# A chunked recurrence on one Trainium2 core: where among a head's scores the next head's decay sums are computed, when the logs are rounded, and which engine takes the queries out of PSUM

## The reference, cut to what matters

```
log_f = logaddexp(log(lb), log1p(-lb) + log_sigmoid(z))     # per token and key dimension
k = (1 - lb) * sigmoid(-z);   q, v from the projection
b = cumsum(log_f)                                            # inside a chunk
A[t, s] = sum_k q[t, k] * k[s, k] * exp(b[t, k] - b[s, k])   # s <= t
o = (q * exp(b)) @ S + A @ v
S = exp(b_last) * S + (k * exp(b_last - b))^T @ v
```

## Time and profile before

| | before |
|---|---|
| median of three runs | 3051.93 us |
| profiled execution, its own time | 3050.5 us |
| its span, first to last instruction | 3048.5 us |
| TensorE busy (matmul) | 3003.0 us, 99% |
| VectorE busy | 1624.6 us, 53% |
| ScalarE busy | 1112.0 us, 36% |
| GpSimd busy | 59.5 us, 2% |
| mean granted TensorE clock | 0.996 |
| chain that ended last | PE 84%, DVE 9%, ACT 5% |

### The profile page before, as it was taken

How to read it: one execution, slowest core, us unless ns; L and a number is a source line. 1 busy time by engine, 2 the same in 40 slices (tenths; PEclk the granted TensorE clock), 3 DMA queues, 4 the chain that set the end, 5 groups by cost and what they waited for, 6 DMA issues and landing times.

```text
span 3048.5 us, 33745 instructions
## 1 busy us (share of the span) xinstructions
PE 3003.0 (99%) x14426; PEld 2479.1 (81%) x14426; DVE 1624.6 (53%) x1880; ACT 1112.0 (36%) x1321; POOL 59.5 (2%) x68
## 2 busy tenths in 40 slices
PE   8999999999999999999999999999999999999998
PEld 6888878888888888888788888888888888788886
DVE  4555555556545466464544555554465564545445
ACT  5535445354322236333432223322236334422222
POOL 0000000000000000200000000000000200000000
PEclk9999999999999999999999999999999999999999
DMA  4121221212233223113222222222232023222221
GB/s 146 52 83 46 88 96 42 83 49 97 97 105 112 97 100 110 41 56 137 81 98 93 93 95 96 97 97 97 97 112 101 22 83 125 82 97 94 90 94 68
DMA packets 41925, 270.56 MB, mean 89 GB/s; under 512 B 5776, under 2 KB 6032, under 8 KB 10544
## 3 DMA queue, kind: packets, MB, share of 16 engines
q1 hardware_dynamic: 41776, 268.40, 25.5%
HBM read 266.22 MB, written 2.10 MB: 88 GB/s over the span
## 4 chain that ended last, share of the span: by engine, by line
PE 84%; DVE 9%; ACT 5%; issue 1%; DVEq 1%; DMA 0%; SPq 0%; ACTq 0%
PE PS L245 24%; PE PS L247 24%; PE PS L246 24%; DVE w_lo L230 4%; ACT w_hi L222 3%; DVE XT L1521 2%; PE PS L2061 1%; PE PS L1145 1%; PE PS L1278 1%; PE PS L652 1%; PE PS L2307 1%; PE PS L2338 1%; PE PS L2041 1%; PE PS L1267 1%; PE PS L710 1%
## 5 line engine op out<-in xcount | busy, mean ns | idle before, releaser
L222 ACT ACTIVATE w_hi<-w_raw 128x2048 fp32r<-128x2048 f32 x241 | 461.3, 1914 | 1202.2 <-PE PS L247 1200.2
L230 DVE TENSOR_TENSOR w_lo<-w_raw,w_hi 128x2048 fp32r<-128x2048 f32 x241 | 552.2, 2291 | 381.8 <-ACT w_hi L222 380.8
L245 PE MATMUL PS<-uh_b,w_hi 128*128 128x512 f32 x1312 | 511.7, 390 | 0.0
L247 PE MATMUL PS<-uh_b,w_lo 128*128 128x512 f32 x1312 | 510.6, 389 | 0.0
L246 PE MATMUL PS<-ul_b,w_hi 128*128 128x512 f32 x1312 | 510.5, 389 | 0.0
L245 PE MATMUL PS<-uh_a,w_hi 128*128 128x512 f32 x800 | 314.0, 393 | 3.6 <-DVE ul_a L572 2.2
L245 PE MATMUL PS<-w_hi,uh_a 128*128 128x512 f32 x768 | 306.1, 399 | 9.2 <-DVE ul_a L305 7.6
L247 PE MATMUL PS<-uh_a,w_lo 128*128 128x512 f32 x800 | 311.4, 389 | 0.0
L246 PE MATMUL PS<-ul_a,w_hi 128*128 128x512 f32 x800 | 311.4, 389 | 0.0
L247 PE MATMUL PS<-w_hi,ul_a 128*128 128x512 f32 x768 | 300.6, 391 | 0.0
L246 PE MATMUL PS<-w_lo,uh_a 128*128 128x512 f32 x768 | 300.5, 391 | 0.0
(11 more groups left out here) (331 smaller groups left out, 3687.9 us busy)
## 6 DMA issues: line engine op xcount, KB each, us to landing
w_raw<-in_weights SPq DMA_DIRECT2D x241, 1024.0 KB, 4.9
XT<-in_xT SPq DMA_DIRECT2D x8, 256.0 KB, 5.9
mem_raw<-in_mem SPq DMA_DIRECT2D x2, 1024.0 KB, 4.8
out<-XT SPq DMA_DIRECT2D x8, 256.0 KB, 2.0
bands<-in_bands SPq DMA_DIRECT2D x2, 768.0 KB, 6.4
mask_numbers<-in_masks SPq DMA_DIRECT2D x1, 1152.0 KB, 8.3
w_raw<-in_weights SPq DMA_DIRECT2D x4, 256.0 KB, 5.3
p_raw<-in_pT SPq DMA_DIRECT2D x2, 512.0 KB, 3.4
```

The source lines that it names most:

```text
L222: act.activation(self.hi[g % 2][:], self.raw[g % 2][:], ACT.Copy).then_inc(self.hi_done.sem, 1)
L230: dve.tensor_tensor(self.lo[g % 2][:], self.raw[g % 2][:], self.hi[g % 2][:], ALU.subtract).then_inc(self.lo_done.sem, 1)
L245: pe.matmul(out, sh, mh, start=first, stop=False)
L247: return pe.matmul(out, sl, mh, start=False, stop=last)
```

## The change

1. **Logs rounded early.** ScalarE rounds the logs inside the projection, after the weight block g0+7 and before it takes `U`, into a new tile `LFhi` that lies where `m.mix` will be. Inside `PoolAndStates` it no longer does so, and VectorE takes the remainder as soon as the last projection block is done.
2. **Queries.** The one VectorE multiplication from PSUM is replaced by four ScalarE copies, one for each bank, and one multiplication from SBUF to SBUF by VectorE after the keys' multiplications. The log sums of chunk c wait for copy c.
3. **Tiles of the coming head's sums among the scores.** Tile 2 of sums(h+1) stands after unit 2 of scores(h), tile 3 after unit 4. Before scores(0) only tiles 0 and 1 of sums(1) are computed; after outputs(h) come turn_keys(h+2) and tiles 0 and 1 of sums(h+2).
4. **States.** VectorE takes the states in the middle of weigh(0), before its fifth level.

```diff
@@ MixerProjection.scalar
         w.split_hi(act, g0 + 7)
+        act.wait_ge(*self.lf.at(1))
+        act.activation(m.LFhi[:, :, 0:DA], m.LF[:], ACT.Copy).then_inc(self.lf_hi.sem, 1)
         w.wait_used(act, g0 + 5)
@@ MixerProjection.vector
         w.split_lo(dve, g0 + 10)
-        w.wait_used(dve, g0 + 9)
-        dve.tensor_tensor(m.Q[:], k.PS[:, 4:8, :], k.R[:].unsqueeze(1).to_broadcast(full), ALU.mult).then_inc(self.qread.sem, 1)
@@ PoolAndStates.scalar
-        act.wait_ge(*self.proj.lf.at(1))
         act.wait_ge(*self.tables.arrived.at(16))
         k.w.wait_used(act, self.proj.g0 + 9)
-        act.activation(uh[:, 0:NT, :], m.LF[:], ACT.Copy).then_inc(self.lf_hi.sem, 1)
-        act.activation(uh[:, 6, 0:P], m.after, ACT.Copy)
-        act.activation(uh[:, 4:6, :].rearrange("p a n -> p (a n)"), m.level, ACT.Copy).then_inc(self.lf_hi.sem, 1)
+        act.activation(uh[:, 6, 0:P], m.after, ACT.Copy).then_inc(self.tables_hi.sem, 1)
+        for h in range(HH):
+            act.activation(m.Q[:, h, :], k.PS[:, 4 + h, :], ACT.Copy).then_inc(self.proj.qread.sem, 1)
+        act.activation(uh[:, 4:6, :].rearrange("p a n -> p (a n)"), m.level, ACT.Copy).then_inc(self.tables_hi.sem, 1)
@@ PoolAndStates.vector
-        dve.wait_ge(*self.lf_hi.at(1))
-        dve.tensor_tensor(self.u[1][:, 0:NT, :], m.LF[:], self.u[0][:, 0:NT, :], ALU.subtract).then_inc(self.lf_lo.sem, 1)
+        dve.wait_ge(*self.proj.lf_hi.at(1))
+        k.w.wait_used(dve, self.proj.g0 + 9)
+        dve.tensor_tensor(self.u[1][:, 0:NT, :], m.LF[:], m.LFhi[:, :, 0:DA], ALU.subtract).then_inc(self.lf_lo.sem, 1)
...
             dve.tensor_tensor(m.Kp[:, c, :], m.Kp[:, c, :], m.K[:, c, :], ALU.mult).then_inc(self.kp.sem, 1)
+        dve.wait_ge(*self.proj.qread.at(HH))
+        dve.tensor_tensor(m.Q[:], m.Q[:], k.R[:].unsqueeze(1).to_broadcast([P, HH, SEQ]), ALU.mult)
+        dve.drain()
@@ PoolAndStates.tensor
-        pe.wait_ge(*self.proj.qread.at(1))
-        pe.wait_ge(*self.lf_hi.at(2))
+        pe.wait_ge(*self.tables_hi.at(1))
         pe.wait_ge(*self.lf_lo.at(1))
         for c in range(NT):
-            pe.matmul(k.PS[:, 4 + c, :], uh[:, 6, 0:P], uh[:, c, :], start=True, stop=False)
+            pe.wait_ge(*self.proj.qread.at(c + 1))
+            pe.matmul(k.PS[:, 4 + c, :], uh[:, 6, 0:P], self.lf_hi_of(c), start=True, stop=False)
@@ Recurrence.vector
             for n in range(LEVELS):
+                if h == 0 and n == 4:
+                    self.states.take_states(dve)
...
         weigh(0)
-        self.states.take_states(dve)
@@ Recurrence.tensor
-        def sums(h):
-            for c in range(NT):
+        def sums(h, tiles):
+            for c in tiles:
...
                 i.then_inc(self.scored.sem, 1)
+                if h + 1 < HH and unit in (2, self.UNITS - 1):
+                    sums(h + 1, (2,) if unit == 2 else (3,))
...
-        sums(0)
+        pe.wait_ge(*self.states.tables_hi.at(2))
+        sums(0, range(NT))
...
-        sums(1)
+        sums(1, (0, 1))
         for h in range(HH):
             scores(h)
-            if h + 2 < HH:
-                turn_keys(h + 2)
...
             outputs(h)
             if h + 2 < HH:
-                sums(h + 2)
+                turn_keys(h + 2)
+                sums(h + 2, (0, 1))
```

More of the change, by code:

```diff
@@ L27 @@
 NH = 8
+PAIRS = NH // 2
 ROPE = 16
@@ L1646, in __init__ @@
         self.lf, self.pooled, self.pool_copied = sig("mixer_lf", 1), sig("mixer_pooled", 4), sig("mixer_pool_copied", 4)
-        self.qread, self.hnorm = sig("mixer_qread", 1), sig("mixer_hnorm", 1)
+        self.qread, self.hnorm, self.lf_hi = sig("mixer_qread", NT), sig("mixer_hnorm", 1), sig("mixer_lf_hi", 1)
     def sync(self, sp):
@@ L1813, in __init__ @@
         self.k, self.m, self.proj, self.u, self.tables = k, m, proj, u, tables
-        self.lf_hi, self.lf_lo, self.state_read = sig("states_lf_hi", 2), sig("states_lf_lo", 1), sig("states_state_read", NT - 1)
+        self.tables_hi, self.lf_lo, self.state_read = sig("states_tables_hi", 2), sig("states_lf_lo", 1), sig("states_state_read", NT - 1)
         self.mapped, self.mapped_read, self.suffix = sig("states_mapped", 4), sig("states_mapped_read", 4), sig("states_suffix", NT)
@@ L1842, in vector, with lf_hi_of @@
             dve.tensor_tensor(m.Kp[:, c, :], m.Kp[:, c, :], m.K[:, c, :], ALU.mult).then_inc(self.kp.sem, 1)
+        dve.wait_ge(*self.proj.qread.at(HH))
+        dve.tensor_tensor(m.Q[:], m.Q[:], k.R[:].unsqueeze(1).to_broadcast([P, HH, SEQ]), ALU.mult)
+        dve.drain()
+    def lf_hi_of(self, c):
+        return self.m.LFhi[:, c, 0:DA]
     def take_states(self, dve):
@@ L2039, in sums @@
                 for half in range(2):
-                    for x in (uh, ul):
-                        i = pe.matmul(k.PS[:, 2 * (c % 2) + half, :], x[:, c, h * P:(h + 1) * P],
-                                      uh[:, 4 + half, :], start=x is uh, stop=x is ul)
+                    bank = k.PS[:, 2 * (c % 2) + half, :]
+                    pe.matmul(bank, self.states.lf_hi_of(c)[:, h * P:(h + 1) * P], uh[:, 4 + half, :], start=True, stop=False)
+                    i = pe.matmul(bank, ul[:, c, h * P:(h + 1) * P], uh[:, 4 + half, :], start=False, stop=True)
                 i.then_inc(self.summed.sem, 1)
@@ L2453, in second_memory @@
     mem.top = at
+    m.LFhi = mem.put("LF_hi", [P, NT, D], F32R)
+    mem.top = at
     m.lb, m.e = mem.put("lb", [P, 2 * DA]), mem.put("lb_exp", [P, 2 * DA])
```

## The result

The changed kernel takes 3079.26 us in the median of four runs (3078.23 to 3081.87), the kernel before 3051.65 in four. The ratio is 1.0093, with a 95% interval from 1.0076 to 1.0111: 27.6 us slower. The forecast was 3072.7, with 20.8 us added to the profiled execution of before, and a range of 3058 to 3084. The execution profiled here took 3081.87 us, the longest of its four, and 31.4 more than the one of before (3050.5).

A forecast was written before the change was run, and what follows sets the result against it. TensorE, busy 99% of the span, was taken as the bound. 13.0 us for two layers plus 9.0 for the clock less 1.2 gave +20.8 on 3050.5, so 3071.3; the median, 1.4 higher, 3072.7; range 3058 to 3084.

The forecast's parts named there:

- Start (edits 1 and 2): Start of the mixer: early rounding and copied queries let the first E come earlier; gain 0.9 us, between 0 and 1.1.
- States (edit 4): Head 0's weighing: with states after four levels, GpSimd finishes beneath them; VectorE needs 8.2 us, not 10.0, gain 1.8.
- The loop on VectorE: Heads 1 to 3: weighing waits for tile 3 and meets GpSimd; periods 16.75 and 17.1 us, +6.5 a layer.
- D: Extra time of a weighing when VectorE and GpSimd multiply SBUF with SBUF together: 4.0 us, head 0 against head 3.
- The clock: TensorE's clock falls behind its 3.4 us idle in heads 1 to 3: 1.5 us each, 9.0 for six, bounds 0 to 3.
- Sum: Whole kernel: 13.0 for two layers, 9.0 for low clock, less 1.2 for the old fall: +20.8 us.
- Range: Whole run: from 3058 us (D 3.3, clock at full level) to 3084 (3 us each fall, larger D in part).
- the clock holds: TensorE in the loop: clock stays up or falls only where TensorE waits anyway; 3063.7 us, chance 0.18.
- the engines don't meet: Weighing in the loop: GpSimd lags or gives way, D is 0, periods 13.2; 3042 us, chance 0.10.
- they meet by half: Weighing in the loop: VectorE wins most turns, D near 2; about 3052 us, no change, chance 0.07.
- blocking rule: Weighings: an undisturbed GpSimd multiplication of 0.73 us is added to each of seven, D 5.1; 3079 us, chance 0.05.

The follow-up runs named there:

- the filled version: Changed kernel with 12, 12 and 18 more 512-column matmuls, results unused, between units 1 and 2 of heads 1, 2 and 3; 3061.25 us, ratio 1.0034.
- GpSimd at three levels: Changed kernel with GpSimd multiplying levels 0 to 2 whole, one column of levels 3 to 6, in heads 1 to 3; 3063.74 us, ratio 1.0050.

## Why the prediction was right, and where its sizes were off

The mechanism and the sign held; that the time came out inside the range is in part luck, as the sum below shows. By the steps of the prediction:

- **Start (edits 1 and 2)**: 0.9 forecast; 1.1 where the clock held. Right, and the rounding cost nothing in its new place: ScalarE's idle ahead of its block there is 4.91 us in place of 6.73.
- **States (edit 4)**: 1.8 forecast on VectorE, and there it is: from the weighing's start to keep 8.0 us (1262.09 to 1270.08), 8.2 forecast, 10.0 before. Without the third edit it is worth 0.07 on the path. With all edits the first outputs of the second layer come 3.3 us earlier than with the tiles alone (26.37 against 29.64), and 1.1 of that is the start's; the 2.1 that are left go to the states by subtraction only, as no run has the tiles and the states without the start. That the two edits lean on each other was not said: the tiles freed TensorE, the states freed VectorE.
- **The loop on VectorE**: keep starts 9.37, 9.74 and 9.83 us after the outputs, forecast 9.75; the seven and the last take 6.9, forecast 6.96, the row of head 0. With the clock held the periods were 16.1 to 16.5 and 17.0, forecast 16.75 and 17.1. GpSimd's part in it is shown by taking its work away: 13.05. By the rule that the prediction drew from the Trainium skill ("SBUF — State Buffer", section "Who interferes with whom"), full blocking with D at 5.1, keep would have started 10.8 after the outputs; the rows show 9.37 to 9.83, so here too only part of the other's time is excluded. The blocking for a whole instruction stands on that page of the Trainium skill beside VectorE's two-port modes; of an instruction with two SBUF inputs it says only that it contends.
- **The clock, the term that was mis-sized**: 1.5 us for each of six heads. That the clock falls at the idle was right in five of six heads; in the second layer's last it fell 2.5 us sooner, behind a wait of 1.31. But it stayed low for 6.8, 10.4 and 10.0 us in the first layer, where I took the 3.5 of the one fall in the second layer of before; the other row that I had, 6 us after an idle of 3.03, was nearer. And the rate of loss was taken from the diagonal's busy time, 1.13 to 1.95, a factor of 1.7, while sixteen 64-column instructions take 3.41 from start to start (1287.70 to 1291.11) in place of the 1.82 that 6.36 for 56 gives, a factor of 1.9. Set against the filled version's periods (16.1 to 16.5, and for both last heads the 17.0 of the first layer), the six cost 2.9, 4.5, 4.2, 3.8, 3.9 and 3.3, 22.6 in all in the profiled execution, not 9.0. The stated upper bound of 3 for one was passed in five of six.
- **Sum**: 13.0 less 2.7 (starts 1.0 and periods 1.7 better than forecast), 22.6 and -1.2 give 31.7, the 31.75 between the profiled executions. That it closes is no proof, since the 22.6 are read from the same periods; the proof is the filled version. In the medians the loss is 27.6. With the clock at its measured size and the rest as forecast, the profiled execution would have come to 3050.5 + 13.0 + 22.6 - 1.2 = 3084.9, above the range's 3084; the two errors lie on opposite sides.
- **Range**: its lower end was added up wrongly. D 3.3 with the clock holding gives 8.8 less 1.2 over 3051.9, that is 3059.5 and not 3058.

The rival *the clock holds* is refuted by the windows; its number of 3063.7 is nearly met by the run that held the clock in all heads but one, 3061.25. The rival *the engines don't meet* is refuted by the rows of VectorE and GpSimd; its 3042 stands as 3046.55 in the run without GpSimd. Its last heads, forecast at 13.1, took 15.6 with a low clock, which accounts for the difference. The rival *they meet by half* is refuted by the same rows. The rival *blocking rule* has the number that came out, 3079 against 3079.26, but not the mechanism: D measured 3.98 (6.94 less 2.96) and not 5.1, and the clock made up the rest.

Left open: when exactly the clock falls. It fell behind waits of 0.60, 0.85, 1.12 and 1.31; in the changed kernel the same wait before units 0 and 1 of the last head was followed by a fall in the second layer (1.31, scores 4.88) and not in the first (1.29, scores 3.76); and it held through many waits of 0.6 among the same scores. No run varied the waits alone, so nothing is claimed on what it takes.

## What to carry to other kernels

Moving a tile into a gap moves its consumers too: ask which engines the last piece of an operand releases, and whether they then multiply SBUF with SBUF at the same moment; here one row of the old kernel, the only head in which both had started together, gave the price to 0.1 us. Fill a gap with work whose consumers are far off, and look at what the head loses from which that work was taken. And price a new wait of TensorE by the clock behind it as well, from the longest low stretch on record, not the shortest; here even the 6 us on record give, with the factor of 1.9, 2.8 for a head and 17 for six, against 22.6.

## What the runs showed of the hardware that I had not expected

Nine useless 512-column matmuls a layer, some 2 us of TensorE's time each layer, made a kernel some 4 to 6 us faster (from 3047.15 to 3041.45; by the ratios to the kernel before, 0.9993 to 0.9979, 4.3), and 42 a layer made another 18 us faster. Low stretches of the clock lasted 10.4 us with TensorE busy from end to end (the window of 10.40 above has 10.40 busy), and longer: in the last head with GpSimd at three levels, second layer, the stretch from 2452.20 to 2464.20 has a clock of 0.50 with 11.91 of its 12.00 us busy. TensorE ran on at the lower level although it was busy.
